# Moving the operands of the matmuls to other places in SBUF: spaces behind the split panels, a wider pitch for u

## The chip, the cores and the metric

One core of one Trainium2 chip runs the whole program in one launch. The metric is the time of one execution on the device in microseconds. The kernel before was timed three times: 2003.85, 2005.51 and 2006.26 us, median 2005.51.

## What is computed

Two blocks of transformer layers, one behind the other, on one sequence of 256 tokens with 1024 channels, batch 1, all in float32. Each block has two layers.

```python
def reference(x, p, ...):
    x = first_block(x, p, w_in, ..., w_ple)          # 2 x _layer
    return second_block(x, c_2, ada_w_2, ..., final_norm_2)

# _layer: h = x @ w_in; three attentions on slices of h (moba, MLA, differential), each with its gate silu(z)
g = jax.nn.sigmoid(x @ w_m + b_m); ga, gb, gc = jnp.split(g, 3, axis=-1)
merged = ga * (ya @ w_a) + gb * (yb @ w_b) + gc * (yc @ w_c)
r = ALPHA * x + merged @ w_o
r = r + jax.nn.sigmoid(r @ w_pg) * (p_i @ w_p)
return _layernorm(r, ln_g, ln_b)

# second_block, each layer: modulated rmsnorm, swiglu (2816 hidden channels), mixers, swiglu
u = modulate(rmsnorm(h, norm_ffn1[l]), mod[:, :, 0], mod[:, :, 1])
h = h + 0.5 * (1.0 + mod[:, :, 2]) * swiglu(u, ffn1_wg[l], ffn1_wu[l], ffn1_wd[l])
proj = u @ w_in[l]                                    # retention, stick-breaking, mamba2
mixed = jnp.concatenate([y_ret, y_sb, y_ssm], axis=-1) @ w_out[l]
```

With 256 tokens every weight is used once, on few columns. The weights are about 387 MB in all, and every dense product is one stream of weight tiles against the same activations.

## The kernel before

**Panels.** The dense weights are cut into panels of at most 128 x 2048 float32 (1 MB), listed by `plan()` in the order of use: 8 chunks of 128 input rows by 256 output columns for most, 2 chunks by 1024 columns for the last product of a feed-forward (`wd`) and for `mix_out`. A panel is loaded by a DMA of SP into one of four raw buffers `weights0` to `weights3`. ScalarE rounds it to float32r, the high part (line 899), and VectorE subtracts to get the low part (line 905); both go to one of three buffers `weights_split0` to `weights_split2`, high part first, low part 8192 bytes behind it. Panels take the three buffers in turn.

**A product.** Activations are kept in the same two parts, [partition, chunk, part, token]: `x`, `y` and `p` in the first block, `u` and `y2` in the second. `parts()` writes every 128 x 128 weight tile against 256 tokens as three matmuls, the product of the two low parts left out: (weights high, x high) on line 753, (weights high, x low) on line 754, (weights low, x high) on line 755. Each is one LDWEIGHTS of 128 columns and one MATMUL of 256 columns. In the feed-forwards `u` has two columns more, 258 in all, which carry the shift. 13,800 of the 14,952 matmuls are of these three lines. In `tensor_tokens` (values of the attentions) and for `m_dt` the roles are swapped: the activations are loaded as weights and the panel streams past.

**Order.** `Order` writes one list of steps for all engines. The panels are prepared two ahead of their use (`AHEAD`). In the feed-forwards a pair of hidden blocks takes three panels, `wg`, `wu`, `wd`, 48 matmuls each, with nothing else on TensorE between them; `vector_pair` and `scalar_pair` work on the pair before. Between them VectorE computes the modulations (line 885). In the first block and in the mixers the products fill the time of the attention steps, which go back and forth between TensorE, ScalarE and VectorE.

**Places in SBUF.** The tensors are laid behind one another in the order in which the code makes them, each rounded up to 32 bytes; `weights0` starts at byte 16512 of a partition. By place the texts mean the address in a partition modulo 512 bytes. From the sizes in the code:

```
tensor                       address   place      bytes
weights0 .. 3                  16512   128        8192 each
weights_split0, 1, 2           49280   128 each   16384 each
h                             101248   384        8192
x     chunk and part 1024     114368   192        16384
p     chunk and part 1024     187072   192        4096
y     chunk and part 1024     191168   192        18432
u     part 1032, chunk 2064   114368   192        16512   high part of chunk c: 192 + 16 c, low part: 200 + 16 c
square_sum                    130880   320        1024
factors                       131904   320        1032
y2    chunk and part 1024     132960   352        12288
hidden0, hidden1              145248   352, 384   2064 each
```

A panel of 256, 128, 384, 512 or 1024 columns has rows of whole 512 bytes, so all its tiles start at the place of its buffer. One panel has not: `("b_ckvr", l, 1)` has 160 columns, so the tiles of its chunks start at 128, 256, 384, 0, 128, ... in turn.

`square_sum` holds the sum of squares that GpSimd adds up (line 2439) for the norm ahead of a feed-forward; TensorE reads it in `tensor_norm`. `hidden` is the ring of two buffers for the gated hidden blocks.

Of the kernel before, what the change touches and what calls it, by code (L numbers as in the profile page):

```python
# [19 lines left out]
F32R = mybir.dt.float32r  # L20
# [4 lines left out]
P = 128  # L25
T = 256
TB = T // P
D = 1024
DC = D // P
# [36 lines left out]
SLOT = 2048  # L66
RAW_SLOTS = 4
SPLIT_SLOTS = 3
# [4 lines left out]
def columns(sizes):  # L73
    at, out = 0, {}
    for name, n in sizes:
        out[name] = at
        at += n
    return out, at
# [558 lines left out]
class Program:  # L637
    def __init__(self, nc, a, out, whole):
# [29 lines left out]
        self.pairs = self.new_ring([both[1], both[0]])  # L668
        self.scores, self.turned = self.new_ring(banks[4:6]), self.new_ring(banks[6:8])
        self.raw = self.new_ring([self.tile(f"weights{i}", [P, SLOT]) for i in range(RAW_SLOTS)])  # L670
        self.split = self.new_ring([self.tile(f"weights_split{i}", [P, 2, SLOT], F32R) for i in range(SPLIT_SLOTS)])
        self.const = {"both": self.tile("constants", [P, columns(CONST_SIZES["both"])[1]])}
        self.small = self.tile("small_parameters", [P, SMALL_N])
        self.h = self.tile("h", [P, DC, T])
# [978 lines left out]
    def second_tiles(self):  # L1653
        sb = lambda name, shape, dtype=F32: self.tile(name, shape, dtype, self.stack)
        b = self.b = {}
        b["u_shift"] = sb("u", [P, DC, 2, T + 2], F32R)
        b["u"] = b["u_shift"][:, :, :, 0:T]
        b["square_sum"] = sb("square_sum", [P, 1, T])
        b["factors"] = sb("factors", [P, T + 2])
        b["y"] = sb("y2", [P, HIDDEN_BLOCKS, 2, T], F32R)  # L1660
        hidden = [sb(f"hidden{i}", [P, 2, T + 2]) for i in range(2)]
        self.hidden = self.new_ring(hidden)
        self.scaled = self.new_ring([h[:, j, 0:T] for h in hidden for j in range(2)])
        b["tmp"] = self.two(hidden[0][:, :, :])[:, 0:2 * T]
        for n in ("r_q", "r_k", "r_g", "m_z"):
            b[n] = sb(n, [P, 4, T])
        b["y_r"] = b["r_q"]
        for n in ("r_v", "s_v"):
            b[n] = sb(n, [P, TB, 512])
        b["squares"] = sb("squares", [P, DC, T])  # L1670
        b["s_q"], b["s_k"] = b["squares"][:, 0:4, :], b["squares"][:, 4:8, :]
        xbc_in = sb("xbc_in", [P, XBC // P * (T + TAPS - 1)])
        b["xbc_in"] = xbc_in[:, :].rearrange("p (c t) -> p c t", c=XBC // P)
        b["xbc"] = sb("xbc", [P, XBC // P, T])
        b["up"] = self.two(b["xbc"][:, :, :])[:, 0:2 * (T + 2)].rearrange("p (j t) -> p j t", j=2)
        b["m_v"] = xbc_in[:, 0:1024].rearrange("p (b n) -> p b n", b=TB)
        b["y_m"] = xbc_in[:, 1024:2048].rearrange("p (c t) -> p c t", c=4)
        stick = xbc_in[:, 0:3 * TRI].rearrange("p (i n) -> p i n", i=3)
        b["dt"] = sb("dt", [P, 6, 2 * MH])
        b["cum"] = sb("cum", [P, 3, MH])  # L1680
        b["neg_a"] = sb("neg_a", [P, MH])
        b["cb"] = sb("keep_then_cb", [P, MG, TRI])
        b["coef"] = sb("coef", [P, 2, DC])
        self.const["second"] = sb("constants_second", [P, columns(CONST_SIZES["second"])[1]])
        work = [sb(f"work{i}", [P, TRI]) for i in range(3)]
        self.maps = self.new_ring(work)
        self.diagonal = work[0][:, 0:P]
        self.maps_t = self.new_ring([sb(f"weights_t{i}", [P, TRI]) for i in range(4)])
        b["stick_work"] = [w[:, :] for w in work] + [stick[:, 0, :]]
        b["stick_keep"] = [b["cb"][:, i, :] for i in range(2)] + [stick[:, 1 + i, :] for i in range(2)]  # L1690
# [890 lines left out]
```

## Time and profile before

| | |
|---|---|
| median of three runs | 2005.51 us |
| the profiled execution | 2002.46 us, of it 2001.2 us span |
| TensorE matmuls busy | 1893.1 us, 95% |
| TensorE weight loads busy | 1819.0 us, 91% |
| VectorE busy | 1372.0 us, 69% |
| ScalarE busy | 954.4 us, 48% |
| GpSimd busy | 63.3 us, 3% |
| DMA engines | mean 195 GB/s |
| granted TensorE clock | 0.978 of 2.4 GHz |

Matmuls are pipelined: a MATMUL of 256 columns is shown with 0.28 us, but the next one starts 0.11 to 0.12 us after it. What one matmul costs in a full stream is the distance between two starts, and so the distances are read from the timeline here, by a first and a last row and the number of matmuls between them, and not from the column of durations.

### The profile page before, as it was taken

The numbers are of one execution on the slowest core, as the hardware profiler recorded it, in microseconds if no ns is written. First come the engines' busy times: TensorE is split into PE (matmuls) and PEld (weight loads), VectorE is DVE, ScalarE is ACT, GpSimd is POOL, SyncE is SP. The second block draws the span as 40 slices with busy tenths as digits, with TensorE's granted clock in tenths as the row PEclk, the third lists the DMA queues.
The fourth block names the chain that finished last, engine by engine and source line by source line (L and its number), as shares of the span: only waits on it lengthen the run. The fifth ranks groups of instructions, "written<-read, shape, count | busy, mean of one in ns | idle before, by whom it ended". The sixth has DMA issues, their size and how long they took to land.

```text
span 2001.2 us, 34162 instructions
## 1 busy us (share of the span) xinstructions
PE 1893.1 (95%) x14952; PEld 1819.0 (91%) x14952; DVE 1372.0 (69%) x1955; ACT 954.4 (48%) x1318; POOL 63.3 (3%) x76
## 2 busy tenths in 40 slices
PE   7998988899899898999999999999999999999998
PEld 7987888899788887999999889999999999799998
DVE  5667676666766767776775867767777776866555
ACT  5564454455644545434455435445444446344443
POOL 0000100000001001000000000001000000010000
PEclk9999999989999998999999999999999999999999
DMA  7453446464453554666455344665665455335551
GB/s 302 171 200 148 159 184 222 182 234 153 184 190 116 224 212 169 254 243 239 185 196 221 117 163 179 251 245 240 241 256 239 163 218 208 129 141 190 180 179 63
DMA packets 59285, 389.70 MB, mean 195 GB/s; under 512 B 6656, under 2 KB 9472, under 8 KB 15232
## 3 DMA queue, kind: packets, MB, share of 16 engines
q1 hardware_dynamic: 59136, 387.52, 50.6%
q8 instruction: 117, 1.92, 0.4%
q14 instruction: 32, 0.26, 0.0%
HBM read 386.45 MB, written 1.05 MB: 194 GB/s over the span
## 4 chain that ended last, share of the span: by engine, by line
PE 67%; DVE 21%; ACT 10%; issue 1%; DMA 0%; POOL 0%; SPq 0%; DVEq 0%; ACTq 0%
PE banks L753 17%; PE banks L754 16%; PE banks L755 16%; DVE weights_split L905 7%; PE bank L755 4%; PE bank L754 4%; PE bank L753 4%; ACT weights_split L899 4%; ACT map L1340 1%; DVE weights L885 1%; DVE xbc L2297 1%; DVE map_stat L1528 1%; ACT map L1346 1%; PE bank L820 1%; PE bank L831 1%
## 5 line engine op out<-in xcount | busy, mean ns | idle before, releaser
L905 DVE TENSOR_TENSOR weights_split<-weights,weights_split 128x2048 fp32r<-128x2048 f32 (+2 forms) x306 | 656.8, 2148 | 337.8 <-ACT weights_split L899 337.1
L753 PE MATMUL banks<-u,weights_split 128*128 128x258 f32 (+1 forms) x2016 | 578.3, 287 | 17.2 <-DVE weights_split L905 6.6
L899 ACT CAST weights_split<-weights 128x2048 fp32r<-128x2048 f32 (+2 forms) x306 | 542.5, 1775 | 80.2 <-PE bank L755 50.6
L754 PE MATMUL banks<-u,weights_split 128*128 128x258 f32 (+1 forms) x2016 | 575.6, 286 | 0.0
L755 PE MATMUL banks<-u,weights_split 128*128 128x258 f32 (+1 forms) x2016 | 572.5, 284 | 0.0
L753 PEld LDWEIGHTS banks<-u,weights_split 128*128 128x128 f32 x2016 | 384.6, 191 | 21.6 <-DVE weights_split L905 8.2
L755 PEld LDWEIGHTS banks<-u,weights_split 128*128 128x128 f32 x2016 | 387.9, 192 | 0.0
L754 PEld LDWEIGHTS banks<-u,weights_split 128*128 128x128 f32 x2016 | 386.3, 192 | 0.5 <-issue 0.5
L753 PE MATMUL banks<-x,weights_split 128*128 128x256 f32 x1056 | 302.9, 287 | 15.0 <-DVE weights_split L905 9.8
L754 PE MATMUL banks<-x,weights_split 128*128 128x256 f32 x1056 | 297.0, 281 | 0.0
L755 PE MATMUL banks<-x,weights_split 128*128 128x256 f32 x1056 | 296.9, 281 | 0.0
L753 PEld LDWEIGHTS banks<-x,weights_split 128*128 128x128 f32 x1056 | 200.3, 190 | 22.8 <-DVE weights_split L905 11.5
L885 DVE CUSTOM_DVE_ANT_0 weights<-weights,cond,small_parameters 128x1024 f32<-128x1024 f32 x160 | 204.5, 1279 | 0.1
L753 PE MATMUL bank<-y,weights_split 128*128 128x256 f32 x720 | 202.6, 281 | 0.0
L755 PE MATMUL bank<-y,weights_split 128*128 128x256 f32 x720 | 202.4, 281 | 0.0
L754 PE MATMUL bank<-y,weights_split 128*128 128x256 f32 x720 | 202.4, 281 | 0.0
L754 PEld LDWEIGHTS banks<-x,weights_split 128*128 128x128 f32 x1056 | 200.5, 190 | 0.3
L755 PEld LDWEIGHTS banks<-x,weights_split 128*128 128x128 f32 x1056 | 200.4, 190 | 0.0
L753 PEld LDWEIGHTS bank<-y,weights_split 128*128 128x128 f32 x720 | 135.8, 189 | 0.0
L755 PEld LDWEIGHTS bank<-y,weights_split 128*128 128x128 f32 x720 | 135.8, 189 | 0.0
L754 PEld LDWEIGHTS bank<-y,weights_split 128*128 128x128 f32 x720 | 135.7, 189 | 0.0
L753 PE MATMUL banks<-y,weights_split 128*128 128x256 f32 (+1 forms) x448 | 131.0, 292 | 3.4 <-ACT b_k L925 3.4
(320 smaller groups left out, 2561.1 us busy)
## 6 DMA issues: line engine op xcount, KB each, us to landing
weights<-in_weights SPq DMA_DIRECT2D x262, 1024.0 KB, 6.9
weights<-in_ada SPq DMA_DIRECT2D x80, 1024.0 KB, 4.8
weights<-in_weights SPq DMA_DIRECT2D x36, 512.0 KB, 5.5
weights<-in_weights SPq DMA_DIRECT2D x4, 576.0 KB, 5.3
constants_second<-in_constants_second SPq DMA_DIRECT2D x1, 1792.0 KB, 9.9
weights<-in_weights SPq DMA_DIRECT2D x2, 640.0 KB, 7.5
h<-in_x SPq DMA_DIRECT2D x2, 512.0 KB, 5.1
out<-xbc SPq DMA_DIRECT2D x4, 256.0 KB, 2.1
```

Of the source, the lines that this page charges most:

```text
L753: pe.matmul(out, left[0], right[0], start=start, stop=False, **more)
L754: pe.matmul(out, left[0], right[1], start=False, stop=False, **more)
L755: return pe.matmul(out, left[1], right[0], start=False, stop=stop, **more)
L820: last = pe.do.matmul(sums[:, 0:some * T], self.k("ones"), rhs, start=k == 0, stop=k == chunks - 1)
L831: last = pe.do.matmul(bank[:, at:at + P], inverse[:, i:i + 1].to_broadcast([P, P]), self.k("ident"), start=True, stop=True)
L885: dve.do.tensor_tensor_reduce(rows, rows, self.cond[:, :], 1.0, bias, ALU.mult, ALU.add, self.mods[:, col:col + 1]).then_inc(*self.dve_wro ...
L899: act.do.copy(split[:, 0, 0:n], raw[:, 0:n]).then_inc(*self.act_wrote.inc(("weights", key)))
L905: dve.do.tensor_tensor(split[:, 1, 0:n], raw[:, 0:n], split[:, 0, 0:n].bitcast(F32), ALU.subtract).then_inc(*self.dve_wrote.inc(("weights" ...
L1340: act.do.activation(probs[:, lo:hi], probs[:, lo:hi], ACT.Exp, bias=st[:, i:i + 1], accum_out=st[:, 2 + i:3 + i]).then_inc(*self.act_wrote ...
L1346: act.do.activation(probs[:, lo:hi], probs[:, lo:hi], ACT.Copy, scale=st[:, 4 + i:5 + i]).then_inc(*self.act_wrote.inc(*[("normalised" if ...
L1528: dve.do.tensor_reduce(st[:, i:i + 1], probs[:, lo:hi], AX.X, ALU.max, negate=True).then_inc(*self.dve_wrote.inc(("maxima", name)))
L2297: dve.do.scalar_tensor_tensor(dst[:, c, :], src[:, c, i:i + T], tap(i), dst[:, c, :], ALU.mult, ALU.add).then_inc(*self.dve_wrote.inc(*[(" ...
```

## The change

It changes addresses and nothing else: no instruction, no wait, no size and no order of work. Behind each of the three split buffers comes an unused tensor of 128 bytes. `u` gets a pitch of 288 elements (1152 bytes) for each part of a chunk in place of 258. `square_sum` loses its own tensor and becomes the first row of `hidden1`, and `factors` is made behind the hidden buffers.

```diff
-        self.split = self.new_ring([self.tile(f"weights_split{i}", [P, 2, SLOT], F32R) for i in range(SPLIT_SLOTS)])
+        split = []
+        for i in range(SPLIT_SLOTS):
+            split.append(self.tile(f"weights_split{i}", [P, 2, SLOT], F32R))
+            self.tile(f"space{i}", [P, 32])
+        self.split = self.new_ring(split)
...
-        b["u_shift"] = sb("u", [P, DC, 2, T + 2], F32R)
-        b["u"] = b["u_shift"][:, :, :, 0:T]
-        b["square_sum"] = sb("square_sum", [P, 1, T])
-        b["factors"] = sb("factors", [P, T + 2])
+        u = sb("u", [P, DC, 2, 288], F32R)
+        b["u_shift"], b["u"] = u[:, :, :, 0:T + 2], u[:, :, :, 0:T]
         b["y"] = sb("y2", [P, HIDDEN_BLOCKS, 2, T], F32R)
         hidden = [sb(f"hidden{i}", [P, 2, T + 2]) for i in range(2)]
+        b["square_sum"] = hidden[1][:, 0:1, 0:T]
+        b["factors"] = sb("factors", [P, T + 2])
```

The places that follow from the sizes: `weights_split0`, `1`, `2` at 128, 256 and 384; all that is made behind them 384 bytes further, so `x`, `p`, `y`, `u` and `y2` at 64. The high parts of `u` stand at 64 and 320 in turn, the low parts at 192 and 448. `y2` starts 18432 bytes behind `u`.

## Rows read from the trace of the kernel before

**Rows 1.** The page: busy time by engine, and the chain that ended last.
```profile
PE 1893.1 (95%) x14952; PEld 1819.0 (91%) x14952; DVE 1372.0 (69%) x1955; ACT 954.4 (48%) x1318; POOL 63.3 (3%) x76
...
PE 67%; DVE 21%; ACT 10%; issue 1%; DMA 0%; POOL 0%; SPq 0%; DVEq 0%; ACTq 0%
```

**Rows 2.** The same chain by line in three stretches: 56:174, 810:980, 990:1150 us.
```profile
by line: DVE weights_split L905 24.8%; ACT weights_split L899 16.8%; ACT map L1340 10.1%; DVE map_stat L1528 8.4%; ACT map L1346 7.8%; DVE map L1522 6.5%; DVE weights L885 5.1%; DVE map L1542 1.9%; issue 1.8%; DVE latents_then_c_qk L1388 1.
...
by line: PE banks L754 22.2%; PE banks L755 22.0%; PE banks L753 21.9%; PE bank L754 11.3%; PE bank L753 11.3%; PE bank L755 11.3%
...
by line: DVE weights_split L905 15.8%; PE banks L753 10.9%; PE banks L755 10.0%; PE banks L754 9.9%; DVE xbc L2297 7.4%; ACT weights_split L899 6.8%; DVE weights L885 5.2%; DVE weights_t L2421 3.3%; ACT work L2015 2.7%; DVE hidden L2397 1.5
```

**Rows 3.** Busy time by engine in two feed-forwards.
```profile
core 0: us, PE busy (x) PEld busy (x) DVE busy (x) ACT busy (x) POOL busy (x), PEclk, DMA share, GB/s
...
810.00:980.00 170.00, 170.00 (x1426) 170.00 (x1426) 122.47 (x125) 71.92 (x62) 0.00 (x0) 1.00 0.62 248
1400.00:1570.00 170.00, 170.00 (x1426) 170.00 (x1425) 121.91 (x123) 73.02 (x64) 0.00 (x0) 1.00 0.62 247
```

**Rows 4.** Timeline of TensorE: start us, us, engine line op; matmuls 1 and 282 of one stream.
```profile
175.40 0.28 PE L753 MATMUL banks<-x,weights_split 128*128 128x256 f32 x1
...
208.50 0.28 PE L755 MATMUL banks<-y,weights_split 128*128 128x256 f32 x1
```

**Rows 5.** Timeline of TensorE in the panel of 160 columns, first layer: matmuls 1, 10, 48.
```profile
23.01 0.28 PE L753 MATMUL banks<-x,weights_split 128*128 128x256 f32 x1
...
24.07 0.28 PE L753 MATMUL banks<-x,weights_split 128*128 128x256 f32 x1
...
28.38 0.28 PE L755 MATMUL banks<-x,weights_split 128*96 128x256 f32 x1
```

**Rows 6.** Timeline in that panel, second layer, and the 237th matmul behind 418.27.
```profile
417.92 0.28 PE L753 MATMUL banks<-x,weights_split 128*128 128x256 f32 x1
...
418.27 0.28 PE L753 MATMUL banks<-x,weights_split 128*128 128x256 f32 x1
418.39 0.28 PE L754 MATMUL banks<-x,weights_split 128*128 128x256 f32 x1
...
445.02 0.28 PE L755 MATMUL banks<-x,weights_split 128*128 128x256 f32 x1
```

**Rows 7.** Timeline in a feed-forward: first matmuls of wu, wd and the next wg.
```profile
1444.81 0.28 PE L753 MATMUL banks<-u,weights_split 128*128 128x258 f32 x1
...
1450.57 0.28 PE L753 MATMUL bank<-y,weights_split 128*128 128x256 f32 x1
...
1456.25 0.28 PE L753 MATMUL banks<-u,weights_split 128*128 128x258 f32 x1
```

**Rows 8.** Timeline in a feed-forward: five matmuls of u in a row.
```profile
1440.13 0.28 PE L753 MATMUL banks<-u,weights_split 128*128 128x258 f32 x1
1440.24 0.29 PE L754 MATMUL banks<-u,weights_split 128*128 128x258 f32 x1
1440.37 0.28 PE L755 MATMUL banks<-u,weights_split 128*128 128x258 f32 x1
1440.49 0.28 PE L753 MATMUL banks<-u,weights_split 128*128 128x258 f32 x1
1440.61 0.28 PE L754 MATMUL banks<-u,weights_split 128*128 128x258 f32 x1
```

**Rows 9.** Timeline in the mixers: first matmuls of two panels on u, 48 apart.
```profile
1598.95 0.28 PE L753 MATMUL banks<-u,weights_split 128*128 128x256 f32 x1
...
1604.66 0.28 PE L753 MATMUL banks<-u,weights_split 128*128 128x256 f32 x1
```

**Rows 10.** Timeline of m_dt: weight loads of 128 columns with only 8 columns streaming.
```profile
1616.99 0.25 PE L753 MATMUL banks<-weights_split,u 128*128 128x8 f32 x1
...
1617.33 0.25 PE L753 MATMUL banks<-weights_split,u 128*128 128x8 f32 x1
```

**Rows 11.** Groups by line and form (of each there are three, L753 to L755).
```profile
L753 PE MATMUL banks<-u,weights_split 128*128 128x258 f32 x1408 | 399.2, 284 | 8.7 <-DVE u L2321 5.3 <-DVE weights_split L905 3.3
...
L753 PE MATMUL bank<-y,weights_split 128*128 128x256 f32 x720 | 202.6, 281 | 0.0
L753 PE MATMUL banks<-u,weights_split 128*128 128x256 f32 x608 | 179.1, 295 | 8.5 <-DVE weights_split L905 3.3 <-DVE u L2367 3.3 <-DVE dt L2379 1.9
```

**Rows 12.** Split work and the square sum: duration ns min/median/max, first and last start.
```profile
L905 DVE TENSOR_TENSOR weights_split<-weights,weights_split x306: 222/2292/3121, 7.3 to 1975.4; 128x2048 fp32r<-128x2048 f32 x130, 128x1024 fp32r<-128x1024 f32 x18, 128x1280 fp32r<-128x1280 f32 x2, 128x1152 fp32r<-128x1152 f32 x2
...
L2439 POOL TENSOR_TENSOR square_sum<-square_sum,squares x24: 729/740/747, 794.0 to 1801.9; 128x256 f32<-128x256 f32 x24
```

## The prediction

> **What bounds the kernel now.** Read the page first: TensorE is busy 95% of the span, and 67% of the chain that ended last is its matmuls [rows 1]. Then the chain by stretch, since an edit of TensorE pays only where TensorE ends last: in a feed-forward all of the chain is matmuls of lines 753 to 755, in the mixers about 31%, in the attentions of the first block next to nothing, there VectorE and ScalarE (split work, maps) end last [rows 2]. In a feed-forward PE has no gap in 170 us, VectorE is busy 72% and ScalarE 42% of them [rows 3]: there only the distance between two matmuls counts.
>
> That distance is not one number, though the instruction is. In the stretch from 175.40 to 208.50 us the matmuls of x and y, 256 columns, follow each other at 33.10 / 281 = 117.8 ns [rows 4]. From 418.27 to 445.02 the same kind of matmuls follow at 26.75 / 236 = 113.3 ns [rows 6]. A third form shows the floor of the weight loads: in m_dt, with 8 columns streaming, 0.34 / 3 = 113, within the rounding 112 ns [rows 10]. So there are two steady rhythms, a long one of 117.8 and a short one of 113.3, and the short one is nearly at the rate of the loads. Within the first block a stream keeps its rhythm: the 282 matmuls of [rows 4] cross several panel borders and keep the long one. A new start behind a wait may fall in either, mostly in the long one.
>
> Where does a stream go over without a wait? In two places of the trace, both in the panel of 160 columns, the only one whose tiles do not all start at place 128 (24 matmuls with 128 columns of weights, then 24 with 96). In layer 1 its first nine matmuls take (24.07 - 23.01) / 9 = 118 ns, the next 38 (28.38 - 24.07) / 38 = 113.4 [rows 5]; the tiles had gone through the places 128, 256, 384 and 0. In layer 2 the rhythm is long up to the last matmul with place 128 and short from 418.27 on, where place 256 begins, and then it stays short for 237 matmuls, through four panels back at place 128 [rows 6]. So with x at 192 the distance weights minus x of -64 keeps either rhythm, a change of the distance by 128 ends the long one and none of the four distances -64, 64, 192, 320 ends the short one.
>
> Reading weights and reading activations thus get in each other's way, or not, by their addresses. The Trainium skill says otherwise: SBUF — State Buffer (section "SBUF: two separate sides") gives TensorE two independent read ports and lets only the port pair of VectorE and GpSimd contend; TensorE never waits. By that rule addresses are free and the time stays; it is the third rival below. The trace does not agree: 117.8 and 113.3 ns for one form at one clock.
>
> **Part by part.** *Split buffers at 128, 256, 384 and x, y, p at 64.* The distances become 64, 192 and 320 by buffer, the three that the long rhythm did not survive, and change by 128 at every panel border. I take 113.3 ns for all streams of x and y that have the long rhythm now. But it counts only where TensorE is on the chain. These are the unbroken stretches: 175 to 208, 295 to 328, 338 to 363 and 365 to 387 us, and the same four in layer 2 (565 to 787), 637 triples or about 1910 matmuls: 1910 x 4.5 ns = 8.6 us. In such a stretch splits of ScalarE and VectorE are on the chain at times; I take three quarters, 6.5 us. In the attentions (56:174 and its like) the gain is absorbed [rows 2]: 0.
>
> *y2 at 64.* In a feed-forward the panel `wd` takes (1456.25 - 1450.57) / 48 = 118.3 ns a matmul [rows 7], at the distance -224. The 720 matmuls for each line [rows 11] less 16 in the mixers make 704 x 3 = 2112. At 113.3: 2112 x 5.0 = 10.6 us, all on the chain.
>
> *u on 1152 bytes.* Now every part of a chunk stands 8 bytes further in place, so the distance is another for each matmul, and so are the times: `wu` takes (1450.57 - 1444.81) / 48 = 120.0 ns [rows 7], and in a row of five 110, 130, 120 and 120 with the rounding of 10 [rows 8]: no steady rhythm is held. Afterwards all distances of u are odd multiples of 64, as those of the 160-column panel were, only that they change every matmul and take in -64 for a quarter. Ends: at best the short rhythm, 113.3 plus two columns at 2.4 GHz, 0.8, = 114.1; at worst no gain or a loss (below). I take 115.5: nearest to the rows at 113.3, with some matmuls lost behind the starts, and because 258 columns were never seen in that rhythm. 1408 x 3 = 4224 matmuls [rows 11] x (119.9 - 115.5) = 18.6 us, at the best end 24.5.
>
> In the mixers u streams with 256 columns, (1604.66 - 1598.95) / 48 = 119.0 ns [rows 9]; 608 x 3 + 96 = 1920 matmuls x 5.6 = 10.8 us, 1.0 more for the 192 of y2. With a TensorE share between 31% (990:1150) and nearly all (the last 45 us, `mix_out`) I take 5 us.
>
> *square_sum in hidden1.* It is written by GpSimd only after the last product before it is added to h and read by the norm before the first gate is scaled, and the hidden buffers are idle then; no wait is added. The 740 ns of an addition [rows 12] read and write no faster elsewhere. The other tensors (factors, raw buffers, h) move in place too. VectorE's split takes 2292 ns for 2048 elements with both inputs at place 128 [rows 12], 1.12 ns each, and hardly differs from one to the next; I put nothing on it. If it grew by 5%, the 28% of free VectorE would hide that in the feed-forwards; in the attentions and mixers, where it is 16 to 25% of the chain [rows 2] of some 1000 us in all, it would cost 0.05 x 0.2 x 1000 = 10 us, and gain as much if it shrank, which two inputs at one place leave open. The split work, DMAs (248 GB/s in a feed-forward, 257 after) and waits are the same in number; 28% of free VectorE and a shorter cycle (17.19 to 16.5 us) leave 25%.
>
> **Sum.** 6.5 + 10.6 + 18.6 + 5 = 40.7 us. The profiled execution has 2002.5 us, so 1961.8; it lies 3.0 under the median of the runs, and the forecast for the median is 1964.8, rounded to 1964. With u at 114.1 and the first block whole it is 1956; with all of the mixers as well 1949.
>
> **Rivals.**
> 1. *Only part locks.* x, y and y2 go to 113.3, but u, with a new distance for every matmul, keeps to about the 119.0 that it has with 256 columns: 17.1 + 4224 x 1.0 = 21 us, so 1984. For it: no row shows 258 columns or a moving operand that changes its place in the short rhythm. Against: the weights' place changed every three matmuls in [rows 6] and the rhythm held.
> 2. *The long rhythm everywhere.* It is drawn at each start and the new distances keep it as -64 does; u and y2 settle at 117.8 (118.6 for 258 columns): 4224 x 1.3 + 2112 x 0.5 + 1 = 8 us, so 1998. Against it stand [rows 5, 6].
> 3. *Addresses don't matter*, by the two ports: the trace's two rhythms come from the order of arrivals alone. 2005, 0. For it: the rhythm of a stream is mostly drawn at a start. Against: y2 and u have other times than x at the same buffers.
> 4. *Slower: u hits the bad distances.* [rows 8] has single distances of 130 beside 110 ns; the mean is 120 only because sixteen places are passed. Afterwards there are four, and if these are bad ones, each matmul of u costs 123, two thirds of the way from the mean to the long one: 4224 x 3 + 1920 x 4 x 0.5 (half on the chain) = 16.5 us more. With x and y2 staying as they are that is 2022. Where they gain their 17.1 us, it comes out slower only if u loses over 17.1 / (4224 + 960) = 3.3 ns on the mean. Against it: odd multiples of 64 were good in [rows 6].
>
> **How the numbers follow.** Forecast 0.53, its own range 1949 to 1976; rival 1: 0.15; rival 2: 0.10; rival 3: 0.08; rival 4: 0.14. Range for eight of ten: 1948 to 2005, which leaves out half of rival 3, most of rival 4, and a little below. A measurement of this kernel tells 0.2% (4 us) from no change. Faster: 0.53 + 0.15 + 0.09 = 0.77; the same 0.10; slower 0.13.
>
> **What would show it.** In the feed-forwards the starts of `wg`, `wu`, `wd` 16.4 to 16.7 us apart per pair instead of 17.19, a panel of `wd` 5.44 us long in place of 5.68, a panel of u 5.5 in place of 5.76. The stretches at 175 and 295 us at 113.3 ns throughout, at the latest after their first panel border. The attentions as long as now. Durations of L905, L899 and L2439 unchanged. The prediction is wrong if a panel of u takes 5.7 us or more, or if the matmuls get shorter and waits for L905 take their place in the feed-forwards.

## The result, and the profile after

The changed kernel takes 1993.7 us (median of 4 runs, 1993.28 to 1994.35) against 2004.95 us for the kernel before (4 runs, 2003.85 to 2006.26) on the same chip: ratio 0.9944, 95% interval 0.9927 to 0.9961. It is faster by 11 us; the forecast was 1964 us, 41 us faster. The profiled execution took 1994.35 us, 8.11 less than the profiled one of before; the account below is of these two.

The page of the changed kernel answers to [rows 1]: first the busy time by engine, then the chain.

```profile
PE 1884.5 (95%) x14952; PEld 1807.3 (91%) x14952; DVE 1371.0 (69%) x1955; ACT 955.4 (48%) x1318; POOL 64.2 (3%) x76
...
PE 65%; DVE 22%; ACT 10%; issue 1%; POOL 0%; DMA 0%; DVEq 0%; ACTq 0%
```

TensorE's share of the chain fell from 67% to 65%; VectorE and ScalarE are as busy as they were. The busy time in the windows of [rows 3] says that the feed-forwards have the same limit as before:

```profile
810.00:980.00 170.00, 170.00 (x1426) 169.87 (x1426) 122.17 (x128) 73.39 (x68) 0.00 (x0) 1.00 0.62 249
1400.00:1570.00 170.00, 170.00 (x1428) 170.00 (x1428) 122.48 (x126) 71.12 (x61) 0.00 (x0) 1.00 0.60 237
```

PE has next to no gap in them (169.87 of 170 us), and 1426 and 1428 matmuls fit where 1426 did: the rate is what it was. The timeline of TensorE there (start us, length, instruction; first matmuls of wg, wu, wd and the next wg) answers to [rows 7]:

```profile
1432.61 0.28 PE L757 MATMUL banks<-u,weights_split 128*128 128x258 f32 x1
...
1438.37 0.28 PE L757 MATMUL banks<-u,weights_split 128*128 128x258 f32 x1
...
1444.13 0.28 PE L757 MATMUL bank<-y,weights_split 128*128 128x256 f32 x1
...
1449.78 0.28 PE L757 MATMUL banks<-u,weights_split 128*128 128x258 f32 x1
```

A panel of u takes 5.76 us, 120.0 ns a matmul, to the digit what it took before. A panel of wd, which streams y2, takes 5.65 / 48 = 117.7 ns instead of 118.3. The cycle is 17.17 us instead of 17.19.

Most of the gain is in the first block. The timeline of the stretch of [rows 4], first matmuls of four panels, whose weights lie in buffers 2, 0, 2 and 0:

```profile
176.48 0.56 PE L757 MATMUL banks<-x,weights_split 128*128 128x256 f32 x1
...
182.97 0.28 PE L757 MATMUL banks<-y,weights_split 128*128 128x256 f32 x1
...
191.44 0.28 PE L757 MATMUL banks<-y,weights_split 128*128 128x256 f32 x1
...
207.76 0.28 PE L757 MATMUL banks<-y,weights_split 128*128 128x256 f32 x1
```

From 182.97 to 191.44 there are 72 matmuls at 117.6 ns, the long rhythm; from 191.44 to 207.76 there are 144 at 113.3, the short one. Two panel borders (buffers 2 to 0 and 0 to 1) left the long rhythm alone; the third, from buffer 1 to buffer 2, ended it. In the other unbroken stretches of the first block that begin long it ends at that border too. Afterwards no border in a stretch brings it back. That is half of the gain there. The other half is in stretches that are short from their start behind a wait; `w_out` with the last `ple`, 216 matmuls in layer 1, first and last start before, then after:

```profile
337.90 0.39 PE L753 MATMUL banks<-y,weights_split 128*128 128x256 f32 x1 [2.08 <-ACT b_k L925]
...
363.33 0.28 PE L755 MATMUL banks<-p,weights_split 128*128 128x256 f32 x1
...
338.97 0.38 PE L757 MATMUL banks<-y,weights_split 128*128 128x256 f32 x1 [2.12 <-ACT b_k L929]
...
363.46 0.28 PE L759 MATMUL banks<-p,weights_split 128*128 128x256 f32 x1
```

25.43 us became 24.49. Of the eight unbroken stretches of the first block none begins short before; afterwards the two of `w_out` and the second of `ple_gate` do.

Split work and square sum keep their durations [rows 12], and VectorE waits for the first half of the split as before (337.1 us in all before, 335.1 after):

```profile
L909 DVE TENSOR_TENSOR weights_split<-weights,weights_split x306: 222/2292/3120, 7.3 to 1967.5; 128x2048 fp32r<-128x2048 f32 x130, 128x1024 fp32r<-128x1024 f32 x18, 128x1280 fp32r<-128x1280 f32 x2, 128x1152 fp32r<-128x1152 f32 x2
...
L2443 POOL TENSOR_TENSOR hidden<-hidden,squares x24: 732/742/753, 788.0 to 1794.3; 128x256 f32<-128x256 f32 x24
```

The 8.1 us by stage, from the starts of the first matmul of each stage, the last feed-forward up to its last product (durations in us, two traces): first block 792.56 before, 786.52 after, so 6.0 gained; the four feed-forwards 782.48 and 781.63, 0.9 gained; the two mixers 413.68 and 412.47, 1.2 gained. Such a duration holds more than the rhythm: TensorE ran at half its clock for 51 us of the first block before and 48 after, in other windows each time, so a difference of 1 us in it says little.

### The profile page after: what moved, and what is told of

It reads as the page before. It is cut to its first block, busy times and chain, and to the rows that moved or that the text cites. A ratio compares the mean times of both kernels' runs of the same rounds, so it can differ in the third digit from the quotient of the medians.

```text
span 1993.0 us, 34162 instructions
## 1 busy us (share of the span) xinstructions
PE 1884.5 (95%) x14952; PEld 1807.3 (91%) x14952; DVE 1371.0 (69%) x1955; ACT 955.4 (48%) x1318; POOL 64.2 (3%) x76
## 4 chain that ended last, share of the span: by engine, by line
PE 65%; DVE 22%; ACT 10%; issue 1%; POOL 0%; DMA 0%; DVEq 0%; ACTq 0%
PE banks L757 16%; PE banks L758 16%; PE banks L759 16%; DVE weights_split L909 8%; ACT weights_split L903 5%; PE bank L759 4%; PE bank L758 4%; PE bank L757 4%; ACT map L1344 1%; DVE weights L889 1%; DVE xbc L2301 1%; DVE map_stat L1532 1%; ACT map L1350 1%; PE bank L824 1%; DVE u L2325 1%
## 5 line engine op out<-in xcount | busy, mean ns | idle before, releaser
L909 DVE TENSOR_TENSOR weights_split<-weights,weights_split 128x2048 fp32r<-128x2048 f32 (+2 forms) x306 | 656.3, 2147 | 335.9 <-ACT weights_split L903 335.1
```

The source lines that it names most:

```text
L909: dve.do.tensor_tensor(split[:, 1, 0:n], raw[:, 0:n], split[:, 0, 0:n].bitcast(F32), ALU.subtract).then_inc(*self.dve_wrote.inc(("weights" ...
```

## Experiments

All times are ratios to the kernel before, run on the same chip as each. "Mean distance" is the mean from one start to the next over all matmuls of a kind in the trace at the full granted clock, without steps of 130 ns and more; it is good to about 0.2 ns. Places and distances (weights minus activations) are mod 512 unless said otherwise.

**The changed kernel beside the others** (no edit), once with three kernels and once more with three others:

> The changed kernel itself, timed beside the next three on one chip, to have its ratio there. By every theory 1989 to 1994 us, 0.993 to 0.996 of the kernel before.

> The changed kernel itself in as many rounds on the same chip: 0.993 to 0.9945 of the kernel before, 1990 to 1994 us, 5 to 8 us behind the one with place 448.

Measured 0.9932 (0.9916 to 0.9949) and 0.9942 (0.9930 to 0.9954), medians 1990.4 and 1991.6 us. The second trace has one thing to learn from, two starts in the stretch from 176 us, 216 matmuls apart:

```profile
180.68 0.28 PE L757 MATMUL banks<-y,weights_split 128*128 128x256 f32 x1
...
205.16 0.28 PE L757 MATMUL banks<-y,weights_split 128*128 128x256 f32 x1
```

24.48 / 216 = 113.3 ns: the same program was in the short rhythm from this stretch's start. So the rhythm with which a stretch begins behind a wait can differ between executions. It is not a free draw: of 44 panels of the first block that begin behind a wait, 31 have one rhythm in all three traces of the changed kernel, 13 don't.

**One operand moved: y2**

```diff
+        sb("pad", [P, 96])
         b["y"] = sb("y2", [P, HIDDEN_BLOCKS, 2, T], F32R)
```

> The changed kernel with one pad of 384 bytes between u and y2, so that the feed-forwards' second products (wd panels, weights in buffer 1 with place 256) read y2 at place 448: weights minus activations is then 320 (mod 512) instead of 192. Theory A (a distance of 320 ends the long rhythm, whatever the buffer): wd panels fall from about 117.8 to 113.4 ns from one matmul to the next, 2112 matmuls save 9 us, time 1984 to 1986 us. Rival B (something else in the third buffer's panels ends it, not the distance): wd panels stay at 117.8, time 1993 to 1994. The u panels stay at 120.0 ns by both.

Ratio 0.9916 (0.9901 to 0.9931), 1985.2 us. First matmuls of wu, wd and the next wg:

```profile
1450.06 0.28 PE L757 MATMUL banks<-u,weights_split 128*128 128x258 f32 x1
...
1455.82 0.28 PE L757 MATMUL bank<-y,weights_split 128*128 128x256 f32 x1
...
1461.27 0.28 PE L757 MATMUL banks<-u,weights_split 128*128 128x258 f32 x1
```

wd takes 5.45 / 48 = 113.5 ns, on the mean too, against 117.4, and the panels of u keep 120.0. Nothing but a place changed, so by this alone places matter. Theory A had the size right; its reason, that a distance of 320 ends the long rhythm, did not survive the next pair.

**All distances alike**

```diff
             split.append(self.tile(f"weights_split{i}", [P, 2, SLOT], F32R))
-            self.tile(f"space{i}", [P, 32])
...
         self.cond = self.tile("cond", [P, D])
+        self.tile("pad", [P, 32])        # 64 in the second kernel
```

> The changed kernel without the spaces, so that all three split buffers lie at place 128, and x, u, y, y2 and p at place 320 (a pad of 128 bytes behind cond): the distance from activations to weights is 320 for every panel of x, y, y2 and p. u keeps its pitch of 1152 bytes and its changing places. Theory A (320 alone ends the long rhythm): the streams over x, y, p and y2 run at 113.3 to 113.8 ns from their first matmuls (x 115.5 before, y 114.7, y2 117.4), which saves some 3000 x 2.0 + 1100 x 1.0 + 2100 x 3.8 ns = 15 us against the changed kernel, time 1977 to 1980 us. Rival B (it is the change of places from panel to panel that ends the long rhythm): no better than x 117.0 of the kernel before, y2 117 to 118, time 1995 to 2003.

> The same as the run before it but with the activations at place 448, so that the distance is 192 for every panel. Theory A: nothing ends the long rhythm, x, y, p and y2 all run at 117.8 ns, time 2000 to 2004 us. Rival B (it is the change of places from panel to panel): the same as at distance 320. Rival C (the distance does not matter once all buffers are alike): both of these kernels within 3 us of each other.

Ratios 0.9953 (0.9938 to 0.9968) and 0.9945 (0.9930 to 0.9959), 1993.6 and 1991.8 us: no theory had both times, except rival C with "within 3 us of each other". Theory A fails. The first with 320, two starts in the first stretch and wd's panel in a feed-forward's middle:

```profile
180.33 0.28 PE L757 MATMUL banks<-y,weights_split 128*128 128x256 f32 x1
...
205.77 0.28 PE L757 MATMUL banks<-y,weights_split 128*128 128x256 f32 x1
```

then the same and a wd panel with 192:

```profile
181.18 0.28 PE L757 MATMUL banks<-y,weights_split 128*128 128x256 f32 x1
...
206.62 0.28 PE L757 MATMUL banks<-y,weights_split 128*128 128x256 f32 x1
...
1444.83 0.28 PE L757 MATMUL bank<-y,weights_split 128*128 128x256 f32 x1
...
1450.28 0.28 PE L757 MATMUL banks<-u,weights_split 128*128 128x258 f32 x1
```

In both, 216 matmuls over six borders stay at 25.44 / 216 = 117.8 ns. Other stretches of the same traces are short from end to end. With one distance everywhere a stretch keeps whichever rhythm it begins in. wd comes out at 113.4 on the mean with 192 and at 117.7 with 320, the other way round than theory A said; why is open, see below.

The equal times hide two opposite differences. The first block takes 785.2 us with 320 and 792.7 with 192 (the other kernels with one distance: 783.1 and 783.7 with 320, 790.1 to 792.6 with 448 or its like); the feed-forwards have it the other way round, by wd. No border ends a long rhythm in either, so in the first block the difference is made where stretches begin. Counted over panels of the first block that begin behind a wait and run in one rhythm: in the three kernels with 320 everywhere (this one and two below) 89 of 135 are short, in the four with 192 or 448 everywhere (the kernel before is one) 48 of 179. So a distance does count by itself, at the start of a stretch.

**Which border ends the long rhythm**

Activations moved on while the spaces stay: `pad` of 96 columns behind `cond` (place 448), or of 64 (place 320).

> The changed kernel with x, u, y, y2 and p all moved on by 384 bytes, to place 448, and the spaces kept: the distances of the three buffers are 192, 320 and 448. Theory C1 (it is the change of distance from 192 to 320 that ends a long rhythm): in the unbroken stretches from 176, 296 and 365 us the long rhythm now ends in panels of the second buffer. Theory C2 (it is the third buffer's place of 384, or its being third): they end in the third buffer's panels as before. y2 (distance 320 in the second buffer) at 113.7 by C1, 117.8 or mixed by C2. Time by C1 1983 to 1988, by C2 1985 to 1994 us.

> The same with the activations at place 320: the distances are 320, 448 and 64. Theory C1: the change from 192 to 320 never comes; if no other change ends a long rhythm, the stretches from 176, 296 and 365 us keep the rhythm they start in, x at 116 to 117.5 ns on average, y2 (distance 448) 117 to 118, time 1994 to 2001 us. Theory C2: the long rhythm ends in the third buffer's panels, x at 115.5, time 1988 to 1994.

Ratios 0.9911 (0.9894 to 0.9929) and 0.9940 (0.9925 to 0.9955). With 448, panels in buffers 0, 1, 2 and 0:

```profile
180.12 0.28 PE L758 MATMUL banks<-y,weights_split 128*128 128x256 f32 x1
...
182.94 0.28 PE L758 MATMUL banks<-x,weights_split 128*128 128x256 f32 x1
...
188.39 0.28 PE L758 MATMUL banks<-y,weights_split 128*128 128x256 f32 x1
...
204.71 0.28 PE L758 MATMUL banks<-y,weights_split 128*128 128x256 f32 x1
```

24 matmuls at 117.5, then 48 at 113.5 and 144 at 113.3: the long rhythm now ends one buffer earlier, at the entry of buffer 1, where the distance goes from 192 to 320. Theory C1 holds, C2 falls. With 320, panels in buffers 1, 2 and 0 of the second stretch:

```profile
298.90 0.28 PE L758 MATMUL banks<-x,weights_split 128*128 128x256 f32 x1
...
304.55 0.28 PE L758 MATMUL banks<-x,weights_split 128*128 128x256 f32 x1
...
310.00 0.28 PE L758 MATMUL banks<-x,weights_split 128*128 128x256 f32 x1
```

117.7 ns in buffer 1, 113.5 in buffer 2. C1 as it was put fails here: the change that ends it is from 448 to 64. The border before, 320 to 448, did not. Both changes that work are 192 to 64 mod 256; those that don't (64 to 192, 320 to 448, 320 to 64) are not. That gave theory M, stated in the expectation of the next run. The time of the second kernel, 1991.4 us, is the one that C2 had; C2 falls by the first.

**Mod 256, and the second half of the change alone**

```diff
-            self.tile(f"space{i}", [P, 32])
+            self.tile(f"space{i}", [P, 64])
```

> The changed kernel with spaces of 256 bytes instead of 128: the buffers lie at places 128, 384 and 128, the activations at 448 (distances 192, 448, 192). Theory M (only distances mod 256 count: 192 and 448 are one and the same, and a long rhythm ends when the distance goes from 192 to 64 mod 256): nothing ends the long rhythm, the stretches from 176 and 296 us keep 117.8 ns to their end, x at 117.0 ns on average, y2 at 113.5 as in the kernel with everything at distance 192; time 1990 to 1993 us. Theory N (a change of places mod 512 between panels is enough): the long rhythm ends within the first three panels of these stretches, x at 115 to 115.5, time 1983 to 1988 us.

For the other kernel the spaces were taken out and all else of the change kept (u's pitch, square_sum's place):

> The other half of the change alone: the kernel before with u's pitch of 1152 bytes, square_sum inside hidden1 and so y2 at place 192, but no spaces (all buffers at place 128, distance 448 everywhere). Theory M (448 is the same as 192): y2 at 113.5 ns as in the kernel with everything at distance 192, x at 117.0 as before, time 1990 to 1993 us, 0.994 to 0.995 of before. Theory N (448 is its own case): y2 at 117.5 to 118, u with 256 columns at 117.8; time 2000 to 2003 us.

Ratios 0.9935 (0.9920 to 0.9951) and 0.9944 (0.9926 to 0.9961), both as theory M said, with y2 at 113.4 ns in both. The first, buffer 1 at the start of the stretch and buffer 0 at its end:

```profile
301.56 0.28 PE L757 MATMUL banks<-x,weights_split 128*128 128x256 f32 x1
...
324.18 0.28 PE L757 MATMUL banks<-y,weights_split 128*128 128x256 f32 x1
```

22.62 / 192 = 117.8 ns over weights places that go from 384 to 128 and back: no border ends it. The second, wd and wg of a feed-forward:

```profile
1442.23 0.28 PE L756 MATMUL bank<-y,weights_split 128*128 128x256 f32 x1
...
1447.67 0.28 PE L756 MATMUL banks<-u,weights_split 128*128 128x258 f32 x1
```

wd at 5.44 / 48 = 113.3 ns, as with 192 everywhere. The time, 1991.3 us, is that of the changed kernel on the same chip (1991.6).

Counted over the traces of all these kernels and of both originals (18 traces), at the borders that a stretch over x, y or p crosses without a wait and with both panels clearly in a rhythm (a mean below 115 ns or above 116.3; `b_ckvr`, `uq` and `ukv` left out, whose tiles lie otherwise): where the distance goes from 192 to 64 mod 256, a long rhythm ended 52 times of 57; from 64 to 192 it ended 0 times of 38, and with the distance unchanged mod 256, 0 of 245. The short rhythm did not end at any of 513 borders.

The feed-forwards have one border of this kind too: the last two panels of wd stand behind one another, in buffers 1 and 2. In the five traces where y2's distance goes from 192 to 64 there with 256 or 258 columns in u, the long rhythm ended 20 times of 20 (117.8 to 113.7 ns in the changed kernel). In the kernel that streams u with 264 columns (below), it ended 0 times of 4. And the rule isn't one for activations that change their place: in u's panels the distance goes from 192 to 64 in every three matmuls, and 256 columns stay at 118.0 ns (below).

**The first half alone**

The kernel before with the spaces, and nothing else of the change:

> The kernel before with the three spaces behind the split panels' buffers alone: x, y and p move to place 64, buffers lie at 128, 256 and 384; u keeps its pitch of 1032 bytes (258 columns) and y2 lies at place 224, square_sum where it was. Theory A (the gain comes from x, y and p with the third buffer's distance of 320): the attentions have the short rhythm as in the changed kernel; of the 11 us some 6 to 9 are there, time 1996 to 1999 us. Rival B (the gain comes from u's pitch in the mixers and from y2): time 2002 to 2005.

Ratio 0.9957 (0.9943 to 0.9970), 1993.5 us: 8.6 us gained, theory A's 6 to 9, though the time lies below its 1996 to 1999. x is at 115.2 ns and y at 114.7, as in the changed kernel; y2 stays at 118.4.

The halves side by side, stage durations in us from the starts in one trace each:

| | first block | feed-forwards | mixers | mean of y2, ns |
|---|---|---|---|---|
| before | 792.6 | 782.5 | 413.7 | 118.3 |
| spaces only | 784.3 | 780.2 | 413.8 | 118.4 |
| pitch only | 790.1 | 772.6 | 412.6 | 113.4 |
| both: the change | 786.5 | 781.6 | 412.5 | 117.4 |
| both, y2 at 448 | 786.4 | 773.3 | 412.8 | 113.5 |
| both, all at 448 | 785.1 | 773.5 | 412.1 | 113.7 |

By the ratios the pitch alone gains 11 us, as much as both, and the spaces alone 9: the pitch 10 us in the feed-forwards, by y2; the spaces 8 in the first block, by x and y. Together, the spaces take the pitch's gain on y2 away (113.4 to 117.4 ns). With them wd's buffer stands at another distance from y2 (192) than the last panel of u has (64), without them both are 192; that this is the reason is not shown, as 64 behind 64 came out either way.

**258 columns**

In the first kernel 23 of 24 matmuls of a group over u stream 256 columns, which leaves most of the shift out of the result; in the second all stream 264. The edit of the first:

```diff
-                last = self.parts(self.pairs.tile(key)[:, at, 0:T + 2], (hi[:, c, cols], lo[:, c, cols]),
-                                  (u[:, c, 0, :], u[:, c, 1, :]), c == order[0], c == order[-1])
+                n = T + 2 if c == order[0] else T
+                do.matmul(out[:, 0:n], hi[:, c, cols], u[:, c, 0, 0:n], start=c == order[0], stop=False)
+                ...                                   # hi x lo and lo x hi with T columns
```

> The changed kernel with the feed-forwards' u streamed as 256 columns instead of 258 in 23 of the 24 matmuls of each group (the two shift columns get only the first product: part of the computation is left out). Theory A (258 columns cannot run faster than 120 ns, wherever they lie): the 4224 matmuls fall to 113.3 to 117.8 ns, 9 to 28 us less, time 1965 to 1985 us. Rival B (it is u's changing places from chunk to chunk that keep it at 120): stays at 119 to 120 ns, time 1990 to 1994.

> The changed kernel with u streamed as 264 columns instead of 258 (six more columns whose results nobody reads). Theory A (a matmul costs 16 cycles of 2.4 GHz more than its columns rounded up to a multiple of 16: 256 gives 272, 258 gives 288): 264 stays at 120.0 ns, time 1993 to 1994. Rival B (the remainder of two columns costs, a multiple of 8 is a better length: 264 + 16 = 280 cycles): 116.7 ns, 14 us less, time 1979 to 1981. Rival C (each column costs): 122.5 ns, 10 us more, 2003 to 2005.

Ratios 0.9917 (0.9903 to 0.9932) and 0.9965 (0.9953 to 0.9976). First matmuls of wu, wd and the next wg with 256 columns:

```profile
1448.54 0.28 PE L1911 MATMUL banks<-u,weights_split 128*128 128x258 f32 x1
...
1454.21 0.28 PE L757 MATMUL bank<-y,weights_split 128*128 128x256 f32 x1
...
1459.86 0.28 PE L1911 MATMUL banks<-u,weights_split 128*128 128x258 f32 x1
```

5.67 / 48 = 118.1 ns, 118.0 on the mean. The run with 264 columns has a mean of 121.5 (1994.7 us, in none of its three ranges). So 2 columns more cost 2.0 ns and 6 more another 1.5: more columns cost more, but not evenly. Theory A's rounding up to 16, by which 258 and 264 cost the same, is out, and what fewer columns give is 2 ns while the places change. The time with 264 is no longer than that because y2 fell to 115.8 ns: its panels are short and long in turn, though no place differs from the changed kernel.

Then u on one place, pitch 1024: with all distances 320, then with the spaces and y2 at 448 (both leave the shift out of the result), and with 258 columns at distance 320 (the shift is multiplied by 0):

```diff
-        u = sb("u", [P, DC, 2, 288], F32R)
+        u = sb("u", [P, DC, 2, T], F32R)
```

> The kernel with distance 320 everywhere, and u without its shift columns: 256 columns in the feed-forwards (one matmul in 24 still has 258) on a pitch of 1024 bytes, so that every chunk of u lies at place 320 too. The shift columns do not enter, so part of the computation is left out. Theory A (it was u's changing places that held 256 columns at 118.0 ns): u runs at 113.3 to 113.8 ns in the feed-forwards and the mixers, 6000 matmuls save 4.5 ns each against the run with 256 columns on the pitch of 1152, 27 us; with the 15 us of distance 320 for the rest some 1940 to 1948 us. Rival B (u's places don't matter, something else in these panels holds it at 118): 1968 to 1973 us.

> u with 256 columns at one place again (64, pitch 1024; shift columns left out, the computation is changed), now with the spaces of the changed kernel (buffers at 128, 256, 384) and y2 at place 448. Theory C (a rhythm is decided where PE starts again after a wait, and is then kept until the distance changes from one panel to the next; the change to the third buffer, from distance 192 to 320, ends a long one): most u panels fall to 113.4 instead of half of them, 5800 x 2.2 = 13 us, y2 falls from 115.6 to 113.5, 4 us: 1953 to 1962 us. Rival D (changes of places between panels do nothing, the rhythms are decided only where PE starts): half and half again, 1968 to 1976 us.

> The kernel of the run with 256 columns of u on one place (all of u at place 320, pitch 1024, all buffers at place 128), but the feed-forwards' matmuls over u stream 258 columns again: each takes the first two columns of what lies behind its chunk, and the shift columns are scaled with 0 (the computation is changed: no shifts enter). Theory A (258 columns hold neither rhythm, wherever u lies): about 120 ns from matmul to matmul, 4000 x 4.4 ns = 18 us more than the 1974 of the run with 256 columns, 1988 to 1993 us. Rival B (258 columns would hold the two rhythms with 256/258 of the steps if the places did not change; the changed kernel's u pitch of 1152 is what kept them out): 114 to 118 ns, 1974 to 1978 us.

Ratios 0.9850 (0.9832 to 0.9868), 0.9830 (0.9813 to 0.9846) and 0.9947 (0.9929 to 0.9965); 1973.9, 1970.2 and 1992.3 us. The first, starts of two u panels (wg, wu) in an early feed-forward and then of wu, wd and the next wg in the third:

```profile
916.27 0.28 PE L1913 MATMUL banks<-u,weights_split 128*128 128x258 f32 x1
...
921.94 0.28 PE L1913 MATMUL banks<-u,weights_split 128*128 128x258 f32 x1
...
1443.17 0.28 PE L1913 MATMUL banks<-u,weights_split 128*128 128x258 f32 x1
...
1448.65 0.28 PE L757 MATMUL bank<-y,weights_split 128*128 128x256 f32 x1
...
1454.09 0.28 PE L1913 MATMUL banks<-u,weights_split 128*128 128x258 f32 x1
```

118.1 ns in the one, 114.2 in the other: u now has the two rhythms, and keeps one for a whole feed-forward: the two of the first layer are long, the two of the second short, wd with them (117.8 and 113.3 ns). So it was the changing places that kept 256 columns out of the short rhythm, as theory A had it, but its time of 1940 to 1948 did not come: half of u stayed long. The time lies just above rival B's 1968 to 1973. With the spaces all four feed-forwards are short:

```profile
1435.34 0.28 PE L1914 MATMUL banks<-u,weights_split 128*128 128x258 f32 x1
...
1440.81 0.28 PE L1914 MATMUL banks<-u,weights_split 128*128 128x258 f32 x1
```

5.47 / 48 = 114.0 ns. In each feed-forward the first panel of wu, in buffer 1, is still at 118 ns and the panel of wg behind it at 114: there the distance goes from 192 to 64. Theory C's share of short panels came, but not its time (1970.2 us instead of 1953 to 1962; rival D had 1968 to 1976). Over all of u the mean fell from 115.6 to 114.7 ns, 5 us of the 13, and y2 at place 448 was now long throughout, 117.8 ns: at each of these borders the short rhythm of u goes over into the long one of wd, 64 behind 64. And with 258 columns on one place:

```profile
1450.26 0.28 PE L1915 MATMUL banks<-u,weights_split 128*128 128x258 f32 x1
...
1456.10 0.29 PE L757 MATMUL bank<-y,weights_split 128*128 128x256 f32 x1
```

5.84 / 48 = 121.7 ns, slower than with changing places. 258 columns hold neither rhythm in any layout that was run.

**A version that beats both**

The kernel with all activations at 448, timed again, beside the changed kernel:

> The changed kernel with x, u, y, y2 and p at place 448 and the spaces kept, timed in more rounds: 0.991 of the kernel before, 1984 to 1987 us; the long rhythm ends in the second buffer's panels and y2 runs at 113.8 ns.

Ratio 0.9914 (0.9900 to 0.9928), 1985.3 us, against 0.9942 (0.9930 to 0.9954) for the changed kernel on the same chip: 6 us better than the change, 18 better than before. One pad of 384 bytes behind `cond` does it.

## Why the prediction was wrong

**Right.** The two rhythms are there, places bear on them, and the first block's term came: 6.0 us of 6.5. L909, L2443 and the waits for the split work stayed as said; the attentions too, within 2 us: from the first `a_v` to the first `gate_a` 120.4 us before and 121.3 to 122.4 in three traces of the changed kernel in layer 1, 116.9 and 116.3 in layer 2. Rival 3 (addresses don't matter) is out: y2 alone, moved by 384 bytes, went from 117.4 to 113.5 ns. The Trainium skill, SBUF — State Buffer (section "SBUF: two separate sides"), lets TensorE's read ports never wait; that addresses are free, as the prediction read from it, these runs contradict. Whether it is a port that waits, no run shows.

**Wrong, u in the feed-forwards (18.6 us, measured under 0.5).** The step was "I take 115.5: nearest to the rows at 113.3". It took the rhythm of 256 columns for 258. 258 never hold it: 120.0 ns with 16 places [rows 7], 120.0 with four, 121.7 with one. The prediction had the number that said so, in rival 1: "no row shows 258 columns or a moving operand that changes its place in the short rhythm". Both halves of that sentence turned out to be causes: at 256 columns changing places give 118.0 ns and one place 114 or 118. The row nearest to a matmul of 258 columns was its own row at 120.0, so no gain at all was at least as likely as the 115.5 that was taken.

**Wrong, y2 (10.6 us, measured 1.9).** The step was "At 113.3: 2112 x 5.0 = 10.6 us", for a place that has distance 192 to wd's buffer. That distance does not by itself make the short rhythm: y2 stayed at 117.4 ns. Within a stretch it is a change that counts, mod 256: 192 to 64 ends a long rhythm, 64 to 192 does not. wd comes behind a panel of u whose last distance is 64 mod 256, and enters at 192; that this kept it long is likely but not shown. The size was right, as six of the runs show (113.4 to 113.7 ns, 9 to 10 us in the feed-forwards), only for other places.

**Wrong in the reading of [rows 5, 6].** The prediction read from the panel of 160 columns that "a change of the distance by 128 ends the long one". It had one panel, in which the distance went through -64, 64, 192 and 320, so both directions were in it. Mod 256 it passes 192 to 64, which is enough. Nor is that panel the only one with other places, as the prediction and the section on places say: the heads in the panels `uq` are 96 columns wide, so their tiles start 384 bytes apart. In layer 2 of the kernel before the first 18 matmuls of `uq`, from 535.60 us on, go from place 128 to place 0 (distance 192 to 64 mod 256) and stay at about 117 ns; these have 96 columns of weights, and the rule above is not shown for them. In the changed kernel a change from 192 to 64 comes at one border in three, and a stretch that begins long stays so up to there.

**Luck in the first block.** Its term was 8.6 us for the unbroken stretches times three quarters, because splits of ScalarE and VectorE are on the chain at times. What came there is, estimated from the lengths of the eight stretches in the two traces, about 5.7 us at equal clock, and for other reasons: some 3.0 from panels behind a border from 192 to 64, some 2.7 from stretches that began short; the rest was lost in panels that stayed long. With 320 everywhere, where no border does anything, the first block took 785.2 us, 1.3 less than in the changed kernel. So its 6.0 us don't prove the reason that the prediction gave.

**Too large, the mixers (5 us, measured 1.2).** u's chunks there have 256 columns but changing places: 118.9 to 117.8 ns on the mean, not 113.3.

The sum as it came: 6.0 + 0.9 + 1.2 = 8.1 us in the profiled executions, 11 in the medians. The 0.9 of the feed-forwards is less than the 1.9 and the 0.2 to 0.4 that the distances of y2 and u give, because the changed kernel's trace has 6.0 us at half the clock there and the other 4.5, and 0.5 us more in steps of 130 ns and above. The measured time lies between rivals 1 and 2, which together had 0.25: u as rival 2 had it and worse, y2 as rival 2, x and y as in the forecast.

**Open.** Which rhythm wd takes when it comes from u's panels can't be told from distances alone: 64 behind 64 (mod 256) was short with y2 alone at 448, long with 320 everywhere, and long with u's 256 columns on one place and the spaces. With 264 columns in u, wd took either in turn at unchanged places. And 5 of 57 changes from 192 to 64 left the long rhythm as it was. Nor is it known what in TensorE or SBUF makes a matmul with 256 columns wait 4.5 ns more in one rhythm. Why 64 gives more short starts than 192 is open too. A layout with both parts of a chunk of u at one place mod 256 (pitch 1280) wasn't tried.

## What to carry to other kernels

Where TensorE streams without a gap, look at the distance between starts of one instruction form, not at its duration: the same form ran at 113.3 or 117.8 ns for hundreds of instructions. If it has two values, try places (a pad of some hundred bytes), and measure each half of such an edit alone: here two halves that gained 9 and 11 us gained 11 to 13 together. What there is to gain is small: the best layout that computes the same gave 18 us of 2003. And don't carry a rhythm from one length of the moving operand to another.

## What the runs showed of the hardware

- fp32r matmuls with 128x128 weights and 256 columns have two steady rhythms, 113.3 and 117.8 ns, and keep one over hundreds of instructions where the activations stay on one place; with places that change from matmul to matmul they took 118.0. 258 columns take 120.0 (121.7 on one place), 264 take 121.5.
- Between two panels of the first block a long rhythm ends where weights minus activations goes from 192 to 64 mod 256 (52 of 57 borders), and at no other border (0 of 283); a short one ended at none of 513. Between two panels of wd it was 20 of 20, but 0 of 4 behind a u of 264 columns. From u to wd a short rhythm did go over into a long one at one distance.
- Which rhythm a stretch starts in can differ from one execution of a program to the next (117.6 and 113.3 ns for the same panels), and depends on the distance: 89 of 135 starts behind a wait were short at 64 mod 256, 48 of 179 at 192.
